# A hybrid decoder step: two small fp32 products written as three products of high and low parts

## The chip, the cores and the metric

The kernel runs on one core of a Trainium2 chip. The metric is the device time of one execution in microseconds (us), the median of the runs of a kernel. Engines are named as the profile names them: PE (TensorE, matmuls), PEld (its weight loads), DVE (VectorE), ACT (ScalarE), POOL (GpSimd), SP (SyncE); ACTq and SPq are the DMA issues of an engine.

## What is computed

One inference step of a decoder with two layers, for 256 tokens of a prompt and 8 single-token requests together: T = 264 columns. The even layer has attention and a short convolution, the odd one gated linear attention and pooling; a SwiGLU block follows each. The change touches two places of the odd layer:

```python
def mixer_odd(h, gla_s0, pool_prev, pool_prev_valid, w_in, w_out, w_alpha_up, b_alpha, gla_gain, w_pool, pool_scale, is_prompt):
    z = h @ w_in
    ...
    zq, zk, zv, zg, zr, zp = jnp.split(z, [o1, o2, o3, o4, o5], axis=-1)
    oc, new_s = gla_mixer(zq, zk, zv, zg, zr, gla_s0, w_alpha_up, b_alpha, gla_gain, is_prompt)
    od, new_pool = pool_mix(zp, pool_prev, pool_prev_valid, w_pool, pool_scale)
    y = jnp.concatenate([oc, od], axis=-1) @ w_out
...
def gla_mixer(zq, zk, zv, zg, zr, s0, w_alpha_up, b_alpha, out_gain, chunked):
    ...
    gk = jax.nn.log_sigmoid((zr @ w_alpha_up + b_alpha).astype(jnp.float32)) / GLA_TAU
...
def pool_mix(u, prev, n_prev, w_pool, scale):
    ...
    for g, w in enumerate(POOL_WINDOWS):
        ...
        outs.append(s / cnt[None, :, None] - ext[:, POOL_BUF:, lo:hi])
    d = jnp.stack(outs, axis=2).astype(u.dtype)
    y = jnp.einsum('btgc,gcd->btgd', d, w_pool).reshape(B, T, POOL_DIM) * scale
```

The gate's up projection is `zr @ w_alpha_up`, 16 to 512. The mix of pooling is the einsum, four groups of 256 to 256.

## The kernel before

**Main products.** All large weights pass in units of two 128-row chunks by 512 columns (`raw`, ring of RING = 4). For each unit ACT copies it to a rounded type (`whi`, fp32r: `split_hi`, L454), DVE subtracts (`wlo` = raw - whi: `split_lo`, L467), and PE does 24 matmuls of 128x128 weights on 264 columns: xh and xl by whi (L583), then xh by wlo (L589). The activations stand as high and low parts too. ACT and DVE split unit n + 3 while PE works on unit n, so they are ahead of PE by AHEAD = 3 units. SP loads unit n when the low part of unit n - 4 is done.

**The odd layer's input projection** is written out by hand as steps s = 0 to 65, each one unit of PE; side work hangs on fixed steps in each engine's own program. Each engine executes its program in order, and semaphores tie them. On PE a step is the unit and then, at some steps: `gate_rank` (s = 10), `dec_outer(s - 40)` (L901, the outer product of a request's key and value, two matmuls), `dec_out` (L911, every second step from s = 42), `pool_mix(c)` (L921, s = 44 to 47 and 52 to 55). On DVE a step is `split_lo`, then `dec_state(s - 40)` (L1720, the state `sgl` of two heads of a request), then the low part of a mix's output (`hl`, L1860) and, at s = 42, 45, 50 and 53, `window_means(g)` (L1735 to L1740), which writes `dmix`. On POOL `window_sums(g)` (L1939) adds the trees of a group's windows: one, two, three and four adds. On ACT a step is `split_hi`, then copies, DMA issues and the high part of a mix's output (`hh`, L1321).

**The two products** are fp32. `gate_rank` multiplies `wup` by `zr` (L813), four matmuls; both have 32 rows, since the 16 columns of the rank stand twice in the weights of steps 8 and 9, as high and low part (is_rank: L449, L464, L957), and `wup` holds the 16 rows twice. `pool_mix` does two matmuls of 128 rows into bank 4, for each of 8 outputs:

```python
                for k in range(2):
                    mm = pe.matmul(ps[:, 4, 0:T], wpool[:, 2 * g + k, m * P:(m + 1) * P], dmix[:, k, :],
                                   start=k == 0, stop=k == 1)
```

The next mix waits for DVE to have taken the last one (pml), and `window_means` of a new group for the mix that reads the old `dmix` (pm_ps).

Of the kernel before, what the change touches and what calls it, by code (L numbers as in the profile page):

```python
# [34 lines left out]
P = 128  # L35
# [99 lines left out]
SGL = 6  # L135


def decoder_step(nc, a, o):
# [6 lines left out]
    with ctx:  # L145
# [92 lines left out]
        zr = put("zr", [32, T], after("attS"))  # L238
        qz = put("qz", [P, GH, NB * NB], after("zr"))
        pst = put("pst", [P, 8, P], after("qz"))  # L240
        assert after("pst") <= end_a, (after("pst"), end_a)
# [19 lines left out]
        wup = put("wup", [32, 512], after("dmix"))  # L261
        sqj = put("sqj", [P, GDV], after("wup"))
        assert after("sqj") <= end_b, (after("sqj"), end_b)
# [73 lines left out]
        gk_ps = sem("gk_ps")  # L337
        zb_ok = sem("zb_ok")
# [91 lines left out]

        def beyond(n, i, step):

            return n + (i * step if isinstance(i, int) else 0) >= U_END

        def split_hi(act, n, i=None, step=0, up=None):
# [12 lines left out]
            if is_rank(n):  # L448
                act.activation(by_rank(whi, n)[:, :, 0:16], by_rank(raw, n)[:, :, 0:16], ACT.Copy).then_inc(hi_done, 1)  # L449
                return  # L450
# [6 lines left out]
        def split_lo(dve, n, i=None, step=0):  # L457
# [4 lines left out]
            if is_rank(n):  # L462
                w = by_rank(whi, n)
                dve.tensor_tensor(w[:, :, 16:32], by_rank(raw, n)[:, :, 0:16], w[:, :, 0:16].bitcast(F32), ALU.subtract).then_inc(lo_done, 1)  # L464
                return
# [101 lines left out]
        def _(pe):  # L567
# [241 lines left out]
            def gate_rank():  # L809
                pe.wait_ge(evac_g, G_ODD + 2)  # L810
                pe.wait_ge(d_odd, 32)
                for h in range(GH):
                    mm = pe.matmul(ps[:, 4 + h, 0:T], wup[:, h * P:(h + 1) * P], zr[:, :], start=True, stop=True)  # L813
# [101 lines left out]
            def pool_mix(c):  # L915
                g, m = divmod(c, 2)
                pe.wait_ge(dmix_ok, g + 1)
                pe.wait_ge(d_wp, 16)
                pe.wait_ge(pml, c) if c else pe.wait_ge(go_ok, 4)
                for k in range(2):  # L920
                    mm = pe.matmul(ps[:, 4, 0:T], wpool[:, 2 * g + k, m * P:(m + 1) * P], dmix[:, k, :],  # L921
                                   start=k == 0, stop=k == 1)
# [22 lines left out]
            for q, (col, s0) in enumerate(zip(ODD_COLS, ODD_FIRST)):  # L945
                G = G_ODD + q
                units = IN_UNITS if col is not None else 2
                for j in range(units):
                    s = s0 + j
                    n = U_ODD + s  # L950
                    if col is None:

                        pe.wait_ge(lo_done, n + 1)
                        for k in range(0, 8, 2):
                            for m, r in enumerate((xh, xl)):
                                for kk in (k, k + 1):
                                    mm = pe.matmul(ps[0:32, 7, 0:T], by_rank(whi, n)[:, kk, 0:32], r[8 * j + kk],  # L957
# [28 lines left out]
                    if 0 <= s - 40 < 16:  # L986
                        dec_outer(s - 40)
                    if s >= 42 and s % 2 == 0 and (s - 42) // 2 < NB:
# [3 lines left out]
                    for half in range(2):  # L992
                        if 44 + 8 * half <= s < 48 + 8 * half:
                            pool_mix(4 * half + s - 44 - 8 * half)
# [8 lines left out]
        def _(act):  # L1003
# [218 lines left out]
            for k in (0, 16):  # L1222
# [32 lines left out]
            for s in range(U_OUT_O - U_ODD):  # L1255
                split_hi(act, U_ODD + s + AHEAD)
                if s == 5:
                    root(2)
                if s == 11:
# [743 lines left out]
```

## Time and profile before

| | us |
|---|---|
| median of 3 runs | 2188.09 (2187.59 to 2188.22) |
| the profiled execution | 2186.03 |
| its span | 2183.9 |
| PE busy in it | 2175.9, 18168 instructions |
| DVE busy | 1211.3 |
| ACT busy | 944.0 |
| POOL busy | 24.3 |

The granted clock of PE is in the top tenth in every slice of the page. A fp32 matmul shows as two PE instructions. The starts of successive matmuls are what counts for PE's time, since the durations of neighbours overlap: matmuls of the main product start 0.12 us apart though one is listed with 0.28 us. The timeline merges alike instructions, and a row's first number is its start.

### The profile page before, as it was taken

What the parts mean: (1) busy time and instruction counts of PE and PEld (TensorE: products, weight loads), DVE (VectorE), ACT (ScalarE), POOL (GpSimd) and SP (SyncE); (2) the same over time, 40 slices, a digit from 0 to 9 for tenths busy, and PEclk for the clock granted to TensorE, in tenths of its full rate; (3) what the DMA queues carried; (4) which work ended last, traced back from release to release, by engine and by line L of the source; (5) the groups of instructions that cost most, each with busy time, mean ns of one, the idle gap of its engine ahead of it and who ended that gap; (6) DMA issues with size and microseconds to landing.
All of it is one profiled execution on the core that took longest, in us unless ns stands there. A gap on an engine that the chain in (4) does not pass through costs nothing.

```text
span 2183.9 us, 43520 instructions
## 1 busy us (share of the span) xinstructions
PE 2175.9 (100%) x18168; PEld 2153.8 (99%) x18168; DVE 1211.3 (55%) x1296; ACT 944.0 (43%) x1055; POOL 24.3 (1%) x35
## 2 busy tenths in 40 slices
PE   9999999999999999999999999999999999999999
PEld 9999999999999999999999899999999999999999
DVE  7777665555555555444465566565555555544443
ACT  7545345443433433443454444454343343433332
POOL 0001000000000000000000020000000000000000
PEclk9999999999999999999999999999999999999999
DMA  7764566566566565556565675556656656566563
GB/s 254 245 171 144 166 184 183 173 193 183 179 185 182 180 185 183 184 176 191 184 204 158 199 234 187 182 171 194 182 180 184 182 180 185 174 192 193 193 191 129
DMA packets 218203, 405.16 MB, mean 186 GB/s; under 512 B 15536, under 2 KB 29616, under 8 KB 217936
## 3 DMA queue, kind: packets, MB, share of 16 engines
q1 hardware_dynamic: 201952, 385.22, 57.5%
q10 hardware_dynamic: 16144, 18.38, 2.5%
q8 instruction: 83, 1.36, 0.2%
q14 instruction: 24, 0.20, 0.0%
HBM read 395.70 MB, written 9.93 MB: 186 GB/s over the span
## 4 chain that ended last, share of the span: by engine, by line
PE 98%; DVE 1%; ACT 1%; DMA 0%; issue 0%; ACTq 0%; DVEq 0%
PE ps L583 63%; PE ps L589 31%; DMA raw<-in_w_in_even 0%; PE ps L921 0%; PE ps L656 0%; PE ps L677 0%; PE ps L666 0%; ACT whi L454 0%; DVE wlo L467 0%; PE ps L874 0%; PE ps L911 0%; PE ps L857 0%; PE ps L878 0%; PE ps L957 0%; PE ps L901 0%
## 5 line engine op out<-in xcount | busy, mean ns | idle before, releaser
L467 DVE TENSOR_TENSOR wlo<-raw,whi 128x1024 fp32r<-128x1024 f32 (+1 forms) x729 | 882.4, 1224 | 788.5 <-ACT whi L454 787.4
L454 ACT ACTIVATE whi<-raw 128x1024 fp32r<-128x1024 f32 (+1 forms) x729 | 761.2, 1055 | 889.2 <-PE ps L589 865.1
L583 PE MATMUL ps<-xh,whi 128*128 128x264 f32 x3904 | 793.6, 284 | 1.0 <-ACT whi L454 1.0
L583 PE MATMUL ps<-xl,whi 128*128 128x264 f32 x3904 | 787.0, 283 | 0.0
L583 PEld LDWEIGHTS ps<-xh,whi 128*128 128x128 f32 x3904 | 599.7, 188 | 9.8 <-issue 6.9
L583 PEld LDWEIGHTS ps<-xl,whi 128*128 128x128 f32 x3904 | 598.9, 188 | 0.0
L589 PE MATMUL ps<-xh,wlo 128*128 128x264 f32 x3904 | 556.5, 283 | 0.0
L589 PEld LDWEIGHTS ps<-xh,wlo 128*128 128x128 f32 x3904 | 504.4, 188 | 0.0
L583 PE MATMUL ps<-hh,whi 128*128 128x264 f32 x1920 | 387.0, 283 | 0.0
L583 PE MATMUL ps<-hl,whi 128*128 128x264 f32 x1920 | 387.0, 283 | 0.0
L583 PEld LDWEIGHTS ps<-hh,whi 128*128 128x128 f32 x1920 | 294.4, 188 | 0.1
L583 PEld LDWEIGHTS ps<-hl,whi 128*128 128x128 f32 x1920 | 294.4, 188 | 0.0
L589 PE MATMUL ps<-hh,wlo 128*128 128x264 f32 x1920 | 270.0, 283 | 0.0
L589 PEld LDWEIGHTS ps<-hh,wlo 128*128 128x128 f32 x1920 | 246.6, 188 | 0.0
L1192 ACT ACTIVATE hh<-ubuf 128x1056 f32 (+1 forms) x22 | 23.9, 1087 | 100.5 <-DVE ubuf L1661 100.5
L1189 ACT ACTIVATE gbuf<-gbuf 128x1056 f32<-128x1056 f32 x22 | 23.9, 1087 | 65.9 <-DVE gbuf L1654 65.9
L1664 DVE TENSOR_TENSOR hl<-ubuf,hh 128x1056 f32 (+1 forms) x22 | 27.7, 1259 | 31.0 <-ACT hh L1192 31.0
L1034 ACT ACTIVATE xh<-x,vec 128x264 fp32r<-128x264 f32 x48 | 20.8, 505 | 36.7 <-DVE x L1624 36.7
L1656 DVE TENSOR_TENSOR ubuf<-ps,rstd 128x1056 f32<-128x1056 f32 x22 | 27.7, 1258 | 12.3 <-PE ps L589 12.3
L1654 DVE TENSOR_TENSOR gbuf<-ps,rstd 128x1056 f32<-128x1056 f32 x22 | 27.7, 1257 | 11.3 <-PE ps L589 11.3
L1380 DVE SCALAR_TENSOR_TENSOR xl<-x,vec,xh 128x264 fp32r<-128x264 f32 x48 | 20.5, 488 | 21.7 <-ACT xh L1034 21.7
L1661 DVE TENSOR_TENSOR ubuf<-ubuf,gbuf 128x1056 f32<-128x1056 f32 x22 | 27.7, 1259 | 2.5
(236 smaller groups left out, 516.2 us busy)
## 6 DMA issues: line engine op xcount, KB each, us to landing
raw<-in_w_gate SPq DMA_DIRECT2D x176, 512.0 KB, 4.0
raw<-in_w_up SPq DMA_DIRECT2D x176, 512.0 KB, 4.3
raw<-in_w_down SPq DMA_DIRECT2D x176, 512.0 KB, 3.9
raw<-in_w_in_even SPq DMA_DIRECT2D x71, 512.0 KB, 4.3
raw<-in_w_in_odd SPq DMA_DIRECT2D x66, 512.0 KB, 3.8
raw<-in_w_out_odd SPq DMA_DIRECT2D x32, 512.0 KB, 4.2
raw<-in_w_out_even SPq DMA_DIRECT2D x16, 512.0 KB, 4.8
raw<-in_w_out_even SPq DMA_DIRECT2D x32, 256.0 KB, 4.2
```

The source lines that it names most:

```text
L454: ins = act.activation(dst, src, ACT.Copy)
L467: ins = dve.tensor_tensor(dst, src, hi.bitcast(F32), ALU.subtract)
L583: pe.matmul(ps[:, bank + t, 0:T], whi[:, s, c:c + P], r[k0 + kk], start=first and kk == 0 and m == 0, stop=False)
L589: mm = pe.matmul(ps[:, bank + t, 0:T], wlo[:, s, c:c + P], yhi[k0 + kk], start=False, stop=last and kk == 1)
L1034: ins = act.activation(xh[c0 + t], x[:, c0 + t, :], ACT.Copy, scale=vec[:, base + c0 + t:base + c0 + t + 1])
L1189: act.activation(gbuf[:, :, :], gbuf[:, :, :], ACT.Silu).then_inc(silu_done, 1)
L1192: act.activation(dst, by_two(ubuf[:, :, :]), ACT.Copy).then_inc(hh_done, 1)
L1380: ins = dve.scalar_tensor_tensor(xl[c], x[:, c, :], vec[:, base + c:base + c + 1], xh[c].bitcast(F32), ALU.mult, ALU.subtract)
L1654: dve.tensor_tensor(gbuf[:, :, :], ps[:, 0:4, 0:T], scale, ALU.mult).then_inc(evac_g, 1)
L1656: dve.tensor_tensor(ubuf[:, :, :], ps[:, 4:8, 0:T], scale, ALU.mult).then_inc(evac_g, 1)
L1661: dve.tensor_tensor(ubuf[:, :, :], ubuf[:, :, :], gbuf[:, :, :], ALU.mult).then_inc(h_ready, 1)
L1664: dve.tensor_tensor(hl[:, at, :, :], by_two(ubuf[:, :, :]), hh[:, at, :, :].bitcast(F32), ALU.subtract).then_inc(hid_done, 1)
```

## The change

- The rank's 16 columns stand three times in steps 8 and 9, each time as high and low part: 96 columns of `whi` instead of 32. `zr` and `wup` have 96 rows (six DMAs of 16 rows instead of two).
- New tiles: `wup3` and `z3` (96 rows, fp32r). ACT copies `wup` and `zr` to them at s = 5 and s = 10 (wu_hi, z_hi), DVE overwrites one third of the rows of each with the low part at s = 6 and s = 10. The gate's four matmuls read these, in fp32r, 96 rows: high by high, low by high and high by low in one product.
- New tiles `wp_hi`, `wp_lo` (the weights of the mix) and `dm_hi`, `dm_lo` (the means). One group of the weights is split at each of s = 43, 44, 48, 49 (POOL_AT and WP_AT); the means at s = 44, 46, 52, 54. Each split is a copy on ACT and a subtraction on DVE, on DVE ahead of `dec_state` of that step.
- A mix is six fp32r matmuls instead of two fp32 ones.
- On PE `pool_mix` stands ahead of `dec_out` of its step, not behind it.

On PE:

```diff
             def gate_rank():
                 pe.wait_ge(evac_g, G_ODD + 2)
-                pe.wait_ge(d_odd, 32)
+                pe.wait_ge(wu_ok, 1)
+                pe.wait_ge(z_ok, 1)
                 for h in range(GH):
-                    mm = pe.matmul(ps[:, 4 + h, 0:T], wup[:, h * P:(h + 1) * P], zr[:, :], start=True, stop=True)
+                    mm = pe.matmul(ps[:, 4 + h, 0:T], wup3[:, h * P:(h + 1) * P], z3[:, :], start=True, stop=True)
...
             def pool_mix(c):
                 g, m = divmod(c, 2)
-                pe.wait_ge(dmix_ok, g + 1)
-                pe.wait_ge(d_wp, 16)
+                pe.wait_ge(dm_ok, g + 1)
+                pe.wait_ge(wp_ok, g + 1)
                 pe.wait_ge(pml, c) if c else pe.wait_ge(go_ok, 4)
-                for k in range(2):
-                    mm = pe.matmul(ps[:, 4, 0:T], wpool[:, 2 * g + k, m * P:(m + 1) * P], dmix[:, k, :],
-                                   start=k == 0, stop=k == 1)
+                for w, d in ((wp_hi, dm_hi), (wp_hi, dm_lo), (wp_lo, dm_hi)):
+                    for k in range(2):
+                        mm = pe.matmul(ps[:, 4, 0:T], w[:, 2 * g + k, m * P:(m + 1) * P], d[:, k, :],
+                                       start=w is wp_hi and d is dm_hi and k == 0, stop=w is wp_lo and k == 1)
```

On ACT:

```diff
-            for k in (0, 16):
+            for k in range(0, 96, 16):
                 act.dma_start(wup[k:k + 16, :], a["w_alpha_up"][0]).then_inc(d_odd, 16)
...
+                if s == 5:
+                    act.wait_ge(d_odd, 16 * 6)
+                    act.activation(wup3[:, :], wup[:, :], ACT.Copy).then_inc(wu_hi, 1)
+                if s == 10:
+                    act.wait_ge(evac_g, G_ODD + 2)
+                    act.activation(z3[:, :], zr[:, :], ACT.Copy).then_inc(z_hi, 1)
...
+                if s in WP_AT:
...
+                    act.wait_ge(d_wp, 16)
+                    act.activation(wp_hi[:, gs, :], wpool[:, gs, :], ACT.Copy).then_inc(wp_h, 1)
+                if s in POOL_AT[::2]:
...
+                    act.wait_ge(dmix_ok, g + 1)
+                    act.activation(dm_hi[:, :, :], dmix[:, :, :], ACT.Copy).then_inc(dm_h, 1)
```

On DVE:

```diff
                 if s == 10:
+                    dve.wait_ge(z_hi, 1)
+                    dve.tensor_tensor(z3[64:96, :], zr[64:96, :], z3[64:96, :].bitcast(F32), ALU.subtract).then_inc(z_ok, 1)
...
+                if s in WP_AT:
...
+                    dve.wait_ge(wp_h, g + 1)
+                    dve.tensor_tensor(wp_lo[:, gs, :], wpool[:, gs, :], wp_hi[:, gs, :].bitcast(F32), ALU.subtract).then_inc(wp_ok, 1)
+                if s in POOL_AT[::2]:
...
+                    dve.wait_ge(dm_h, g + 1)
+                    dve.tensor_tensor(dm_lo[:, :, :], dmix[:, :, :], dm_hi[:, :, :].bitcast(F32), ALU.subtract).then_inc(dm_ok, 1)
                 if 0 <= s - 40 < 16:
                     dec_state(s - 40)
```

DVE at the end of s = 42 to s = 44, of before: the last of the window means (L1740), then for s = 43 and s = 44 a unit's low part (`wlo`) and a state step (`sgl`), then the output of the first mix.

```order
L1740 SCALAR_TENSOR_TENSOR dmix<-small,pst 128x2x8
L467 TENSOR_TENSOR wlo<-raw,whi 128x1024
L1720 SCALAR_TENSOR_TENSOR sgl<-sgl,sqs,ps 128x256 x2
L467 TENSOR_TENSOR wlo<-raw,whi 128x1024
L1720 SCALAR_TENSOR_TENSOR sgl_b<-sgl_b,sqs,ps 128x256 x2
L1860 SCALAR_TENSOR_TENSOR hl<-ps,vec,hh 128x264
```

The same place after the change (L493 is `wlo`, L1763 the state step, L1904 and L1908 the new low parts).

```order
L1783 SCALAR_TENSOR_TENSOR dmix<-small,pst 128x2x8
L493 TENSOR_TENSOR wlo<-raw,whi 128x1024
L1904 TENSOR_TENSOR wp_lo<-wpool,wp_hi 128x512
L1763 SCALAR_TENSOR_TENSOR sgl<-sgl,sqs,ps 128x256 x2
L493 TENSOR_TENSOR wlo<-raw,whi 128x1024
L1904 TENSOR_TENSOR wp_lo<-wpool,wp_hi 128x512
L1908 TENSOR_TENSOR dm_lo<-dmix,dm_hi 128x528
L1763 SCALAR_TENSOR_TENSOR sgl_b<-sgl_b,sqs,ps 128x256 x2
```

Three subtractions stand between the means of group 0 and the point at which PE may read `dm_lo`, and two unit low parts with a state step between them.

DVE at s = 6 to s = 10, of before: the second rank unit's low part, the query's four tiles, low parts, the rank to `zr`, two low parts, and the gate's result.

```order
L464 TENSOR_TENSOR whi<-raw,whi 128x8x16
L1425 TENSOR_TENSOR qg<-ps,rstd 128x264 x4
L467 TENSOR_TENSOR wlo<-raw,whi 128x1024 x2
L1756 TENSOR_TENSOR zr<-ps,rstd 32x264
L467 TENSOR_TENSOR wlo<-raw,whi 128x1024 x2
L1786 TENSOR_SCALAR sqs<-ps,vec 128x264 x4
```

The same place after the change, with the low parts of `wup3` (printed as wup_119) and `z3` (z_103).


```order
L490 TENSOR_TENSOR whi<-raw,whi 128x8x3x16
L1828 TENSOR_TENSOR wup_119<-wup,wup_119 32x512
L1468 TENSOR_TENSOR qg<-ps,rstd 128x264 x4
L493 TENSOR_TENSOR wlo<-raw,whi 128x1024 x2
L1799 TENSOR_TENSOR zr<-ps,rstd 96x264
L493 TENSOR_TENSOR wlo<-raw,whi 128x1024 x2
L1831 TENSOR_TENSOR z_103<-zr,z_103 32x264
L1834 TENSOR_SCALAR sqs<-ps,vec 128x264 x4
```

The new subtraction stands behind the two `wlo`, ahead of the four additions that take the gate's result (L1786, now L1834).

## Rows read from the trace of the kernel before

**Rows 1.** The page, part 1: each engine's busy time, share, instructions.
```profile
PE 2175.9 (100%) x18168; PEld 2153.8 (99%) x18168; DVE 1211.3 (55%) x1296; ACT 944.0 (43%) x1055; POOL 24.3 (1%) x35
```
**Rows 2.** Timeline, PE, s = 10 and the gate: start, duration, engine, line, idle before.
```profile
1125.19 0.41 PE L583 MATMUL ps<-xh,whi 128*128 128x264 f32 x2
...
1128.18 2.04 PE L813 MATMUL ps<-zr,wup 32*128 32x264 f32 x8
...
1133.15 0.40 PE L583 MATMUL ps<-xh,whi 128*128 128x264 f32 x2
```
**Rows 3.** Timeline, ACT and DVE, while PE does s = 10.
```profile
1125.46 1.06 ACT L454 ACTIVATE whi<-raw 128x1024 fp32r<-128x1024 f32 x1 [0.89 <-PE ps L957]
...
1125.75 2.34 DVE L467 TENSOR_TENSOR wlo<-raw,whi 128x1024 fp32r<-128x1024 f32 x2
```
**Rows 4.** Timeline, PE, s = 44 to s = 54: starts of steps, dec_outer, dec_out and mixes.
```profile
1246.93 0.41 PE L583 MATMUL ps<-xh,whi 128*128 128x264 f32 x2
...
1249.82 0.40 PE L901 MATMUL ps<-v,kdiag 72*128 72x256 f32 x2
...
1254.83 1.06 PE L921 MATMUL ps<-dmix,wpool 128*128 128x264 f32 x4
...
1271.53 0.41 PE L583 MATMUL ps<-xh,whi 128*128 128x264 f32 x2
...
1274.75 0.62 PE L911 MATMUL ps<-sgl,qz 128*8 128x256 f32 x8
...
1278.54 0.41 PE L583 MATMUL ps<-xh,whi 128*128 128x264 f32 x2
...
1286.44 1.06 PE L921 MATMUL ps<-dmix,wpool 128*128 128x264 f32 x4
```
**Rows 5.** Timeline, DVE, s = 43 and s = 44.
```profile
1245.78 1.97 DVE L467 TENSOR_TENSOR wlo<-raw,whi 128x1024 fp32r<-128x1024 f32 x1 [0.37 <-ACT whi L454]
1247.67 0.86 DVE L1720 SCALAR_TENSOR_TENSOR sgl<-sgl,sqs,ps 128x256 f32<-128x256 f32 x2
1248.45 1.32 DVE L467 TENSOR_TENSOR wlo<-raw,whi 128x1024 fp32r<-128x1024 f32 x1
```
**Rows 6.** Timeline, POOL, beside Rows 5: the two adds of group 1.
```profile
1245.58 1.09 POOL L1939 TENSOR_TENSOR tree<-ext 128x540 f32<-128x540 f32 x1 [3.12 <-DVE dmix L1740]
1246.74 1.94 POOL L1939 TENSOR_TENSOR tree<-tree 128x536 f32<-128x536 f32 x1
```
**Rows 7.** Groups by form, DVE, 1100 to 1320 us: the subtraction's nearest size.
```profile
L1387 DVE TENSOR_TENSOR sqs<-sqs 128x528 f32<-128x528 f32 x1 | 0.7, 708 | 0.0
```
**Rows 8.** Timeline, DVE, s = 46 and s = 54, the unit's low part.
```profile
1257.96 1.22 DVE L467 TENSOR_TENSOR wlo<-raw,whi 128x1024 fp32r<-128x1024 f32 x1
...
1289.78 1.22 DVE L467 TENSOR_TENSOR wlo<-raw,whi 128x1024 fp32r<-128x1024 f32 x1
```
**Rows 9.** Timeline, DVE, s = 49: low part and state step.
```profile
1271.90 1.22 DVE L467 TENSOR_TENSOR wlo<-raw,whi 128x1024 fp32r<-128x1024 f32 x1
1273.04 0.87 DVE L1720 SCALAR_TENSOR_TENSOR sgl<-sgl,sqs,ps 128x256 f32<-128x256 f32 x2
```
**Rows 10.** Timeline, POOL, s = 49 and s = 52: adds of groups 2 and 3.
```profile
1272.07 1.99 POOL L1939 TENSOR_TENSOR tree<-ext 128x540 f32<-128x540 f32 x1 [23.39 <-DVE pst L1774]
...
1280.71 4.46 POOL L1939 TENSOR_TENSOR tree<-tree 128x536 f32<-128x536 f32 x3
```
**Rows 11.** Timeline, DVE, s = 52: the unit's low part.
```profile
1280.39 1.32 DVE L467 TENSOR_TENSOR wlo<-raw,whi 128x1024 fp32r<-128x1024 f32 x1
```
**Rows 12.** Timeline, the odd layer's start: ACT's DMA issues and first splits.
```profile
1101.21 1.53 ACTq L1235 DMA_DIRECT2D sgl<-in_state_gla  x3
1102.84 2.96 ACT L454 ACTIVATE whi<-raw 128x1024 fp32r<-128x1024 f32 x3 [0.81 <-issue]
```
**Rows 13.** Timeline, PE, start of s = 3 of the odd layer.
```profile
1106.45 0.40 PE L583 MATMUL ps<-xh,whi 128*128 128x264 f32 x2
```
**Rows 14.** Timeline, ACT's DMA issue of a state at s = 44.
```profile
1249.03 1.20 ACTq L1235 DMA_DIRECT2D sgl<-in_state_gla  x1
```

## What the change should do to the time, worked out before it ran

> **What bounds the kernel now.** I read the page's busy times first. PE is busy for 2175.9 of 2183.9 us, in 18168 instructions [rows 1]; that is 0.120 us from one matmul to the next. So PE is the bound everywhere, and what counts of any edit is how long it keeps PE at work or at a wait. I then read the timeline of PE at the two places touched, and beside it DVE, ACT and POOL, since the new products wait for a chain of splits on those. ACT and DVE have spare time on average, but a mean doesn't say whether the split of a value made a moment before is ready when PE arrives; only the order in their queues does.
>
> **The gate, what PE saves.** From the start of unit s = 10 to the start of the unit after s = 11 are 1133.15 - 1125.19 = 7.96 us [rows 2]. Two units of 24 matmuls at 0.12 are 5.76, so the four fp32 matmuls cost 2.20. The four new ones have the form of the main product but for 96 rows; the nearest row with fewer rows, a key-value product of 72 rows, is listed with the same 0.40 for two [rows 4]. I take 0.12 each: 0.48.
>
> **The gate, its new wait.** The unit s = 10 is issued by 1125.19 + 2.88 = 1128.07. DVE's two low parts run to 1125.75 + 2.34 = 1128.09 [rows 3], and the new subtraction on 264 columns stands behind them. Its price: 528 columns take 0.71 [rows 7] and 1024 take 1.22 [rows 8], so about 1.03 ns a column and 0.44 for 264. Successors begin some 0.08 before the listed end of the one ahead (1245.78 + 1.97 against 1247.67 in [rows 5]), so it runs from 1128.01 to 1128.45. ACT's copy to `z3` begins behind its unit at 1126.5 [rows 3] and takes about half of that unit's 1.06, so it is done by 1127.1 and not the last. With 0.1 for the signal and an unhidden weight load (my choice; bounds 0 and 0.3) PE waits 0.5. The gate comes to 1.0 instead of 2.2: **-1.2**.
>
> **The mix, what PE saves.** Steps 44 to 49 take 1271.53 - 1246.93 = 24.60 with four mixes and three dec_out; steps 50 and 51 take 7.01 with one dec_out and no mix [rows 4]. Three times 7.01 is 21.03, so a mix costs 3.57 / 4 = 0.89. Six matmuls at 0.12 are 0.72. Eight mixes save 8 x 0.165: **-1.3**. Moving `pool_mix` ahead of dec_out costs nothing by itself, but the 0.6 of dec_out no longer stands between the unit and the mix, and would have covered as much of each wait below.
>
> **The mix, what it waits for.** The odd mixes of a pair find both operands ready. The first one of each group waits for `dm_lo`. Times are those of the trace of before; a shift of PE moves both sides.
>
> *Group 0, s = 44.* DVE's low part at 1245.78 took 1.97 where the same instruction takes 1.22 elsewhere [rows 5, 8]. POOL's add had started at 1245.58 and ended at 1246.67, and POOL's second add shows 1.94 from 1246.74 but ends 0.93 after DVE's low part, at 1248.68 [rows 6]. So a subtraction and an add that both read SBUF twice exclude each other, and the later one waits: 0.75 here. The Trainium skill says so too (SBUF — State Buffer, Who interferes with whom): a DVE instruction with two SBUF inputs contends with a GpSimd one that reads SBUF, the one issued second blocks until the first is done, and this speaks against new subtractions beside the trees. Now `wp_lo` of group 0 comes at 1247.67, right behind that low part, with POOL's second add already waiting. I take it that POOL goes first. Then `wp_lo` runs effectively from 1248.55, 0.69 long (512 columns), to 1249.24; the state step 0.86 to 1250.02; the low part 1.22 to 1251.17; the second `wp_lo` to 1251.77; `dm_lo` (0.71) to 1252.40, each begun 0.08 early. PE is through its unit and dec_outer at 1249.82 + 0.24 = 1250.06 [rows 4]. Wait 2.34, with 0.15 for signal and load **2.5**.
>
> *Group 1, s = 46.* The chain starts at the mix of s = 45, M = 1254.83 [rows 4], whose end is awaited by ACT and DVE and by the means of group 1. The unit's low part follows at 1257.96 = M + 3.13 [rows 8]. The new mix ends at 0.88 (five starts of 0.12 and 0.28) instead of 1.06, so 0.18 earlier: M + 2.95 to M + 4.17. `dm_lo` ends at M + 4.80. PE is there at M + 0.72 + 2.88 + 0.24 = M + 3.84. Wait 0.96 + 0.15 = **1.1**.
>
> *Group 2, first s = 50.* The fourth `wp_lo` at s = 49 comes at 1273.04, while POOL's first add has been waiting since 1272.07 for the low part of 1271.90 [rows 9, 10]. POOL goes first and is done at 1272.07 + 1.99 = 1274.06; `wp_lo` runs from about 1273.95 to 1274.64, and the state step behind it ends at 1275.42 where it ended at 1273.91. dec_out at 1274.75 needs it [rows 4]: wait **0.75**, on a wait that had 0.8 to spare.
>
> *Group 2, then s = 52.* Now the means are 0.75 ahead of PE, so the low part of the unit isn't held by them but by ACT's own, and I put its end at 1281.2 (at most 1280.39 + 1.32 = 1281.71, as before [rows 11]). POOL's second add for group 3 waits at that moment (before it began at 1280.71 [rows 10]), takes its 0.93, and `dm_lo` runs from 1282.05 to 1282.75. PE is there at 1278.54 + 2.88 + 0.24 = 1281.66 [rows 4]. Wait 1.1 + 0.15 = **1.3**.
>
> *Group 3, s = 54.* As group 1 with M = 1286.44, but the low part stands at 1289.78 = M + 3.34 [rows 4, 8]: wait 1.17 + 0.15 = **1.3**. POOL is done by then.
>
> Sum of the waits: 2.5 + 1.1 + 0.75 + 1.3 + 1.3 = 6.95.
>
> **What is covered.** The four more DMA issues of `wup` stand ahead of ACT's first split of the odd layer. Three issues take 1.53 [rows 12], so four take 2.0 at that pitch, and the split of unit 3 begins at 1104.9 instead of 1102.84 and ends at 1105.9; PE wants it at 1106.45 [rows 13]. It fits, with 0.6 to spare. The wider rank split and the splits of `wup3` lie on engines that are several us ahead of PE there, and `wp_lo` of s = 48 fits into DVE's gap ahead of the state step. I put all of them at nothing; if the cover of the DMA issues fails, it costs what the rival below says. The wider `zr` and the wider rank weights (96 columns where 128 have the same pitch) are nothing either.
>
> **The sum.** -1.2 - 1.3 + 6.95 = +4.4 against the profiled execution's 2186.03: 2190.5. The median of the runs lies 2.1 above that execution, so I forecast 2188.09 + 4.4 = **2192.5**.
>
> **Rivals.**
> *DVE keeps its turn.* If a subtraction that follows another at once goes ahead of POOL's waiting add, `wp_lo` at 1247.67 isn't held. It ends at 1248.36, the state step at 1249.14, the low part (1.32, held a little by the add) at 1250.38, the second `wp_lo` at 1250.99, `dm_lo` at 1251.62: s = 44 waits 1.7. dec_out at s = 50 waits for nothing, and s = 52 for about 1.2 (POOL's adds are later there instead). Waits 1.7 + 1.1 + 1.2 + 1.3 = 5.3, total 5.3 - 2.5 = +2.8: **2190.9**. For it speaks that no row shows two such subtractions in a row with an add waiting, so the order is my inference; against it that in every pair of rows the one that asked first went first.
> *The waits are covered.* If PE finds `dm_lo` ready, only the savings are left, 1.3 + 1.7: **2185.1**. Against it stands that all of DVE's work on the way is listed with its duration; for it only that the chain has many links. It is not a gain that the runs can tell.
> *Slower than this: the DMA issues.* One issue of the same queue took 1.20 [rows 14]. If four 16-row issues took that each, 4.8 in all, the split of unit 3 would end at 1102.84 + 4.8 + 1.06 = 1108.7, 2.2 behind PE's 1106.45: total +6.6, **2194.7**. It decides from 0.64 per issue. Against it: three neighbours took 0.51 each.
>
> **Chances.** The forecast 0.58, DVE keeps its turn 0.22, DMA issues late 0.12, covered 0.04, something else 0.04. About 0.2%, 4.4 us here, is what a measurement can tell from no change, that is 2192.5 at the upper side: the forecast lies on this line, so I give half of its chance to either side. Slower: 0.29 + 0.12 + 0.03 = 0.44. Same: 0.29 + 0.22 + 0.04 = 0.55. Faster by that much has no case, 0.01. The range holds the first two cases with 0.1 to 0.2 of doubt on each of five waits, and most of the third: 2189.9 to 2194.4.
>
> **What would show it.** In the trace after: PE idle ahead of the first mix of s = 44 for 2.3 to 2.6 (1.6 to 1.8 in the rival), of 46, 52 and 54 for 1.0 to 1.4, ahead of one dec_out for 0.7, and ahead of the gate for 0.4 to 0.5, each put down to DVE's `dm_lo`, `sgl` or `z3`; `wp_lo` listed with some 1.6 at s = 43 and s = 49 and 0.7 elsewhere; six mix matmuls 0.12 apart; no idle time at s = 3. Wrong would be a mix without a wait, or a wait on ACT: then my order of links is wrong.

## The result: 8 us slower, more than forecast

| | before, us | after, us |
|---|---|---|
| median of 6 runs | 2187.77 (2187.59 to 2188.22) | 2196.09 (2192.29 to 2198.85) |
| the profiled execution, its span | 2186.03, 2183.9 | 2195.65, 2193.5 |

The ratio is 1.0038, with a 95% interval of 1.0028 to 1.0048. The forecast was 2192.5, in a range of 2189.9 to 2194.4: the sign of the sum was right, its size was not. The changed kernel spreads over 6.6 us, and the six runs of before beside it over 0.6; in the later sessions, with 15 to 27 executions, the kernel before spreads over 3.0 to 3.5 us itself, so at most a spread twice as wide is shown. The changed kernel ran twice more, with 10 and 5 executions; the median of all 21 is 2195.64, 7.8 above the 2187.8 of before.

Parts 1 and 2 of the page after answer to [rows 1]. PE is busy for 3.5 us more and its span is 9.6 longer, so most of the loss is time in which PE stands.

```profile
PE 2179.4 (99%) x18180; PEld 2157.6 (98%) x18180; DVE 1219.9 (56%) x1306; ACT 949.4 (43%) x1065; POOL 25.0 (1%) x35
```

The timeline of PE at the gate and from s = 44 answers to [rows 2, 4] (start, duration, engine, line, names; in brackets the idle time ahead and what ended it; L609 and L615 are the main products, L840 the gate, L928 dec_outer, L938 dec_out, L949 the mix).

```profile
1132.05 0.73 PE L840 MATMUL ps<-z,wup 96*128 96x264 f32 x4 [0.61 <-DVE z L1831]
...
1252.18 0.40 PE L928 MATMUL ps<-v,kdiag 72*128 72x256 f32 x2
1254.79 0.51 PE L949 MATMUL ps<-dm_hi,wp_hi 128*128 128x264 f32 x2 [2.21 <-DVE dm_lo L1908]
1255.14 0.41 PE L949 MATMUL ps<-dm_lo,wp_hi 128*128 128x264 f32 x2
1255.38 0.41 PE L949 MATMUL ps<-dm_hi,wp_lo 128*128 128x264 f32 x2
...
1256.27 0.81 PE L609 MATMUL ps<-xh,whi 128*128 128x264 f32 x2
1256.88 0.64 PE L609 MATMUL ps<-xl,whi 128*128 128x264 f32 x2
1257.32 0.64 PE L609 MATMUL ps<-xh,whi 128*128 128x264 f32 x2
...
1265.94 0.51 PE L949 MATMUL ps<-dm_hi,wp_hi 128*128 128x264 f32 x2 [0.84 <-DVE dm_lo L1908]
...
1282.31 0.62 PE L938 MATMUL ps<-sgl,qz 128*8 128x256 f32 x8 [0.63 <-DVE sgl L1763]
...
1290.46 0.51 PE L949 MATMUL ps<-dm_hi,wp_hi 128*128 128x264 f32 x2 [1.07 <-DVE dm_lo L1908]
...
1300.26 0.51 PE L949 MATMUL ps<-dm_hi,wp_hi 128*128 128x264 f32 x2 [1.05 <-DVE dm_lo L1908]
```

The six waits are where the forecast has them and end by the operations it names. What it doesn't have stands behind the first: successive rows of two matmuls in the next unit start 0.44 us apart (1256.88, 1257.32) instead of 0.24. The windows show it as the granted clock, the column behind POOL's busy time. The first row is of before, the second and third of after:

```profile
1250.00:1300.00 50.00, 50.00 (x402) 44.98 (x402) 34.00 (x67) 18.31 (x25) 11.23 (x7) 1.00 0.86 273
```
```profile
1250.00:1300.00 50.00, 44.47 (x358) 40.71 (x356) 37.98 (x71) 20.18 (x29) 12.94 (x8) 0.97 0.79 254
...
1256.00:1260.00 4.00, 4.00 (x26) 3.73 (x19) 1.72 (x2) 1.26 (x2) 0.00 (x0) 0.57 0.96 329
```

PE stood for 2.2 us, went on at full clock for 1.5, and then had the lower level (granted clock 0.50, that is 1.2 of 2.4 GHz) for the next 3.4.

DVE and POOL answer to [rows 5, 6, 7]: the new low parts, and the two adds of group 1.

```profile
1248.87 1.23 DVE L493 TENSOR_TENSOR wlo<-raw,whi 128x1024 fp32r<-128x1024 f32 x1 [1.10 <-ACT whi L480]
1250.03 1.57 DVE L1904 TENSOR_TENSOR wp_lo<-wpool,wp_hi 128x512 fp32r<-128x512 f32 x1
1251.52 0.86 DVE L1763 SCALAR_TENSOR_TENSOR sgl<-sgl,sqs,ps 128x256 f32<-128x256 f32 x2
1252.30 1.21 DVE L493 TENSOR_TENSOR wlo<-raw,whi 128x1024 fp32r<-128x1024 f32 x1
1253.44 0.68 DVE L1904 TENSOR_TENSOR wp_lo<-wpool,wp_hi 128x512 fp32r<-128x512 f32 x1
1254.04 0.69 DVE L1908 TENSOR_TENSOR dm_lo<-dmix,dm_hi 128x528 fp32r<-128x528 f32 x1
...
1279.89 1.58 DVE L1904 TENSOR_TENSOR wp_lo<-wpool,wp_hi 128x512 fp32r<-128x512 f32 x1
```
```profile
1247.94 1.09 POOL L1996 TENSOR_TENSOR tree<-ext 128x540 f32<-128x540 f32 x1 [3.12 <-DVE dmix L1783]
1249.10 1.94 POOL L1996 TENSOR_TENSOR tree<-tree 128x536 f32<-128x536 f32 x1
```

`wp_lo` takes 1.57 at s = 43 and 1.58 at s = 49, where an add of POOL was waiting ahead of it, and 0.68 at s = 44, where none was. That is the order that the prediction inferred. The place is not the same in every execution, though. In e1, the changed kernel again, ACT's split came later, POOL's second add was already running when the unit's low part came, and the collision fell on that one: 1.86 instead of 1.23, and `wp_lo` behind it was free with 0.68. DVE and POOL there:

```profile
1248.15 1.86 DVE L493 TENSOR_TENSOR wlo<-raw,whi 128x1024 fp32r<-128x1024 f32 x1 [1.64 <-ACT whi L480]
1249.93 0.68 DVE L1904 TENSOR_TENSOR wp_lo<-wpool,wp_hi 128x512 fp32r<-128x512 f32 x1
```
```profile
1247.84 1.08 POOL L1996 TENSOR_TENSOR tree<-tree 128x536 f32<-128x536 f32 x1
```

**Where the time is lost, in numbers.** From the start of dec_outer at s = 44 to that at s = 55 the trace before has 1295.00 - 1249.82 = 45.18 us. The forecast for this stretch, with seven of the eight mixes, is 6.95 - 7 x 0.165 = +5.8. The profiled execution after has +7.39, and the two repeats +10.08 and +10.43. So the executions of one kernel differ here by 3 us, and the experiments ask why.

### The profile page after: what moved, and what is told of

It reads as the page before. It is cut to its first block, busy times and chain, and to the rows that moved or that the text cites. A ratio compares the mean times of both kernels' runs of the same rounds, so it can differ in the third digit from the quotient of the medians.

```text
span 2193.5 us, 43569 instructions
## 1 busy us (share of the span) xinstructions
PE 2179.4 (99%) x18180; PEld 2157.6 (98%) x18180; DVE 1219.9 (56%) x1306; ACT 949.4 (43%) x1065; POOL 25.0 (1%) x35
## 4 chain that ended last, share of the span: by engine, by line
PE 95%; DVE 2%; DMA 1%; ACT 1%; issue 1%; ACTq 0%; POOL 0%; SPq 0%; DVEq 0%; POOLq 0%
PE ps L609 61%; PE ps L615 31%; DMA raw<-in_w_in_even 1%; DVE wlo L493 1%; DMA raw<-in_w_in_odd 1%; ACT whi L480 0%; PE ps L949 0%; PE ps L682 0%; PE ps L703 0%; POOL tree L1996 0%; PE ps L692 0%; PE ps L901 0%; PE ps L884 0%; PE ps L905 0%; DVE dm_lo L1908 0%
## 5 line engine op out<-in xcount | busy, mean ns | idle before, releaser
L493 DVE TENSOR_TENSOR wlo<-raw,whi 128x1024 fp32r<-128x1024 f32 (+1 forms) x729 | 881.7, 1223 | 793.6 <-ACT whi L480 792.4
L609 PE MATMUL ps<-xh,whi 128*128 128x264 f32 x3904 | 796.2, 285 | 0.4 <-ACT whi L480 0.4
L609 PE MATMUL ps<-xl,whi 128*128 128x264 f32 x3904 | 789.8, 283 | 0.0
L609 PEld LDWEIGHTS ps<-xh,whi 128*128 128x128 f32 x3904 | 600.6, 189 | 10.7 <-issue 9.1
L609 PEld LDWEIGHTS ps<-xl,whi 128*128 128x128 f32 x3904 | 600.2, 188 | 0.0
L615 PE MATMUL ps<-xh,wlo 128*128 128x264 f32 x3904 | 556.9, 283 | 0.0
L615 PEld LDWEIGHTS ps<-xh,wlo 128*128 128x128 f32 x3904 | 504.4, 188 | 0.0
L609 PE MATMUL ps<-hh,whi 128*128 128x264 f32 x1920 | 387.5, 283 | 0.0
L609 PE MATMUL ps<-hl,whi 128*128 128x264 f32 x1920 | 387.4, 283 | 0.0
L609 PEld LDWEIGHTS ps<-hh,whi 128*128 128x128 f32 x1920 | 294.2, 188 | 0.1
L609 PEld LDWEIGHTS ps<-hl,whi 128*128 128x128 f32 x1920 | 294.2, 188 | 0.0
L615 PE MATMUL ps<-hh,wlo 128*128 128x264 f32 x1920 | 270.1, 283 | 0.0
L615 PEld LDWEIGHTS ps<-hh,wlo 128*128 128x128 f32 x1920 | 246.5, 188 | 0.0
```

The source lines that it names most:

```text
L493: ins = dve.tensor_tensor(dst, src, hi.bitcast(F32), ALU.subtract)
L609: pe.matmul(ps[:, bank + t, 0:T], whi[:, s, c:c + P], r[k0 + kk], start=first and kk == 0 and m == 0, stop=False)
L615: mm = pe.matmul(ps[:, bank + t, 0:T], wlo[:, s, c:c + P], yhi[k0 + kk], start=False, stop=last and kk == 1)
```

## The experiments

All times are medians of 5 to 11 executions beside the kernel before, whose median was 2187.75 to 2187.91 in the four sessions (e1 to e4; e5 to e7; e8 to e11; e12 and e13). The changed kernel itself had 2193.54 in one session and 2196.91 in another, so differences of less than about 3 us between medians of different sessions say little. "Stretch" is the difference to before from s = 44 to s = 55, as above.

| run | median, us | ratio, 95% | stretch | idle ahead of the mix of s = 44, s = 52 |
|---|---|---|---|---|
| e1 changed kernel again | 2193.54 | 1.0018 to 1.0037 | +10.08 | 2.48, 2.23 |
| e2 gate alone | 2187.11 | 0.9986 to 1.0004 | 0.00 | none |
| e3 pooling alone | 2196.57 | 1.0024 to 1.0048 | +11.69 | 2.48, 3.59 |
| e4 mix behind dec_out | 2191.10 | 1.0009 to 1.0027 | +4.34 | 1.73, 1.69 |
| e5 POOL's adds later | 2191.96 | 1.0010 to 1.0028 | +6.57 | 1.88, 1.35 |
| e6 both DMA pairs later | 2191.22 | 1.0005 to 1.0023 | +4.73 | 1.11, 1.07 |
| e7 gate and mixes later | 2186.69 | 0.9986 to 1.0004 | | none |
| e8 mixes later | 2185.44 | 0.9977 to 0.9995 | | none |
| e9 and z3 first | 2184.67 | 0.9975 to 0.9993 | | none |
| e10 first wait filled | 2196.49 | 1.0023 to 1.0050 | +10.10 | 0.58, 3.62 |
| e11 changed kernel again | 2196.91 | 1.0029 to 1.0056 | +10.43 | 2.48, 2.49 |
| e12 second DMA pair later | 2194.05 | 1.0020 to 1.0041 | +7.60 | 2.48, 1.05 |
| e13 same, wait filled | 2192.91 | 1.0014 to 1.0035 | +6.11 | 0.58, 1.13 |

### The change in its two halves

e1 is the changed kernel unaltered.

> The changed kernel itself, a second time. Waits theory: 2195 to 2196, PE idle about 2.2 us ahead of the first mix of s = 44, 0.8, 1.1 and 1.0 ahead of those of s = 46, 52, 54, 0.6 ahead of the gate and of one dec_out, at the same places again; what lies ahead of the odd layer (3.2 us more than before in the first trace, in code that the change doesn't touch) is chance and should be gone or of another size. Rival, the program as a whole: the 3.2 us ahead of the odd layer are there again.

Its median, 2193.54, is below the 2195 to 2196 expected. It spread from 2192.5 to 2197.9, and its trace has the slow stretch behind s = 44 for longer.

e2 keeps the gate's half only; `pool_mix` is as before and behind dec_out.

```diff
-POOL_AT = (44, 45, 46, 47, 52, 53, 54, 55)
-WP_AT = (43, 44, 48, 49)
+POOL_AT = ()
+WP_AT = ()
```

> The gate's part alone (rank thrice, wup3, z3); pooling's mix is fp32 and behind dec_out, as before. Waits theory: the gate saves 0.9 (four matmuls of 0.12 and a wait of 0.6 in place of 2.2), so 0.9 below the kernel before, about 2186.9, with a spread as small as that of the kernel before (0.6). Rival, any change of the program unsettles its start: 1 to 3 us above the kernel before, spread of some us.

Its row of the gate (PE's timeline):

```profile
1130.71 0.72 PE L840 MATMUL ps<-z,wup 96*128 96x264 f32 x4 [0.44 <-DVE z L1830]
```

From the first rank unit (s = 8) to dec_outer of s = 44 it needs 127.44 us where before needs 128.52: the gate saves 1.08. The median is 0.6 below before, and the interval includes no change.

e3 keeps pooling's half only; `gate_rank`, `zr`, `wup` and their DMAs are as before.

```diff
-                pe.wait_ge(wu_ok, 1)
-                pe.wait_ge(z_ok, 1)
+                pe.wait_ge(d_odd, 32)
                 for h in range(GH):
-                    mm = pe.matmul(ps[:, 4 + h, 0:T], wup3[:, h * P:(h + 1) * P], z3[:, :], start=True, stop=True)
+                    mm = pe.matmul(ps[:, 4 + h, 0:T], wup[0:32, h * P:(h + 1) * P], zr[0:32, :], start=True, stop=True)
```

> Pooling's part alone (split weights and means, six matmuls a mix, mix ahead of dec_out); the rank stands once and the gate is fp32. Waits theory: the five waits less the savings, 5.7, so 2193.5, and 1.5 more where the clock falls behind the long wait of s = 44: 2195.0. If instead the clock falls come from the gate's wait or the front: 2193.5 with a small spread.

It is as slow as the whole change, so the loss is pooling's. In its trace PE waits 3.59 at s = 52, and the clock is low after both long waits.

### What makes the waits

e4 puts `pool_mix` behind dec_out again, as before.

```diff
                         dec_outer(s - 40)
-                    for half in range(2):
-                        if 44 + 8 * half <= s < 48 + 8 * half:
-                            pool_mix(4 * half + s - 44 - 8 * half)
...
                         out_T((s - 60) // 4)
+                    for half in range(2):
+                        if 44 + 8 * half <= s < 48 + 8 * half:
+                            pool_mix(4 * half + s - 44 - 8 * half)
```

> The changed kernel with pool_mix behind dec_out again, as it stood before. Waits theory: dec_out's 0.6 us of work covers as much of each of four waits, so 2.2 to 2.4 below the changed kernel (about 2193.8); 1.5 more below it if the wait at s = 44, then 1.6 instead of 2.2, no longer brings the clock down (2192.3). Rival, the order is of no account because DVE's chain moves along: within 0.5 of the changed kernel.

PE does dec_out while it would have waited, and s = 44 waits 1.73:

```profile
1252.01 0.52 PE L949 MATMUL ps<-dm_hi,wp_hi 128*128 128x264 f32 x2 [1.73 <-DVE dm_lo L1908]
```

No matmul behind it is slow: from the mix's start to the next dec_outer are 1255.74 - 1252.01 = 3.73, the mix and a unit at 0.12 each (3.6) and the step's own 0.1. The order that the prediction put at "costs nothing by itself" is worth 2.4 us beside e1 (2193.5, same session) and 4.5 beside the changed kernel's median over all 21 executions. The cover of 0.6 on each of four waits would be 2.4 already; that the clock stays up is seen in the one trace and is not separable in the medians.

e5 lets POOL's adds wait until the low part beside them is done, so the two never meet.

```diff
                     pool.wait_ge(dmix_ok, g)
+                if g in (1, 3):
+                    pool.wait_ge(dm_ok, g)
+                if g == 2:
+                    pool.wait_ge(wp_ok, 4)
```

> The changed kernel, but POOL's trees of groups 1 and 3 wait until the means of the group before are split (dm_ok), and those of group 2 until all weights are split (wp_ok 4). So no add stands beside the new subtractions. Theory of the shared reads: wp_lo shows 0.7 at s = 43 and s = 49 instead of 1.6, dm_lo 0.7 at s = 52; the waits fall from 2.2 to about 1.0 (s = 44), from 0.6 to 0 (dec_out at s = 50), and about 1 at s = 52; 3 us less in all than the changed kernel, and the clock stays up behind s = 44, 1.5 less again: 2189.5 to 2191. Rival, DVE's queue alone makes the waits: within 1 us of the changed kernel (2193.5 to 2196).

DVE's rows of s = 43 (timeline): neither subtraction is held. The unit's low part starts behind ACT's split after an idle time of 1.68, as in e1 (1.64), and takes 1.23 where e1 has 1.86; `wp_lo` takes 0.69 as there.

```profile
1248.06 1.23 DVE L493 TENSOR_TENSOR wlo<-raw,whi 128x1024 fp32r<-128x1024 f32 x1 [1.68 <-ACT whi L480]
1249.20 0.69 DVE L1904 TENSOR_TENSOR wp_lo<-wpool,wp_hi 128x512 fp32r<-128x512 f32 x1
```

The wait for `sgl` ahead of dec_out at s = 50 (0.63) is gone, and s = 44 is 0.6 shorter than in e1 (1.88, 2.48), the 0.63 that the low part is shorter. This confirms the exclusion as a cause of these waits. The expectation was missed: 2191.96 is above 2189.5 to 2191, and the clock still fell at s = 44. The effect on the median is between 1.6 us (beside e1) and 3.7 (beside all 21 executions), both from other sessions, so its size is open.

e6 moves the two pairs of DMA issues in `pool_rows` (the outputs of pooling's state, `ext` and `pst`) from s = 42 and s = 50 of ACT's program to s = 47 and s = 60.

```diff
-                    if s == 42 + 8 * half:
+                    if s == (47, 60)[half]:
                         pool_rows(half)
```

> The changed kernel, but ACT issues the two pairs of DMAs of pool_rows at s = 47 and s = 60 instead of s = 42 and s = 50. Theory of the uncovered issues (they took 1.0 to 2.7 us a pair from trace to trace, and stand ahead of the splits that the first mixes wait for): the units' low parts at s = 43 and s = 51 start as soon as PE has freed the slot, the wait at s = 52 is 1.1 each time instead of 1.1 to 3.6, median 1 to 1.5 below the changed kernel, and a narrower spread. Rival, the spread is the clock's alone: median and spread as the changed kernel's.

The wait at s = 44 fell to 1.11 from between 2.2 and 2.5, though `wp_lo` took 1.58, and the runs lie closer together (2189.45 to 2192.18). So about half of the longest wait was ACT's: it issues the two DMAs ahead of the split of a unit, the unit's low part on DVE waits for that split, and all new low parts stand behind it. How long an issue takes differs from one execution to the next. First ACT's timeline after, ahead of s = 44 and ahead of s = 52 (L1280 and L1281 are the pair), then the first of the pair ahead of s = 52 in e11 and in e10 (there L1284):

```profile
1245.63 0.58 ACTq L1280 DMA_DIRECT2D out<-ext  x1
1246.24 1.44 ACTq L1281 DMA_DIRECT2D out<-pst  x1
1247.78 1.06 ACT L480 ACTIVATE whi<-raw 128x1024 fp32r<-128x1024 f32 x1 [3.52 <-issue]
...
1283.22 0.52 ACTq L1280 DMA_DIRECT2D out<-ext  x1
1283.78 0.62 ACTq L1281 DMA_DIRECT2D out<-pst  x1
```
```profile
1282.05 2.00 ACTq L1280 DMA_DIRECT2D out<-ext  x1
```
```profile
1280.46 2.40 ACTq L1284 DMA_DIRECT2D out<-ext  x1
```

At s = 52 the pair took 0.52 + 0.62 = 1.14 after (idle 1.07), 0.53 + 1.35 in e1 (idle 2.23), 2.00 + 0.53 in e11 (2.49), 2.40 + 0.53 in e10 (3.62).

### What the clock costs

In e10 PE does 16 more matmuls ahead of the first mix, on 256 columns each, whose result is overwritten; the mix can't start earlier by that.

```diff
+                pe.wait_ge(pml, c) if c else pe.wait_ge(go_ok, 4)
+                if c == 0:
+                    pe.wait_ge(wp_h, 1)
+                    for k in range(16):
+                        pe.matmul(ps[:, 4, 0:256], wp_hi[:, k % 2, 0:P], wp_hi[:, 0, 0:256], start=True, stop=True)
                 pe.wait_ge(dm_ok, g + 1)
                 pe.wait_ge(wp_ok, g + 1)
-                pe.wait_ge(pml, c) if c else pe.wait_ge(go_ok, 4)
```

> The changed kernel, and ahead of the first mix, while PE would wait for the low part of the means, 16 matmuls (128x128 on 256 columns, their result overwritten) of 0.12 us each, 1.9 us in all. Nothing is taken off the path: dm_lo comes when it comes. Theory (the clock falls because PE stood still): the wait of 2.2 to 2.5 becomes 0.3 to 0.6 behind the filling, the granted clock stays at full level and the eight slow pairs behind the mix are gone: 1.5 below the changed kernel run beside it, about 2193. Rival (the clock falls for another reason, as what ACT, DVE and POOL do at that place, or would have risen anyway): slow pairs behind the mix as before and no difference, or slower by what the filling overshoots, 0 to 0.3.

> The changed kernel itself once more, beside the one with the filled wait: 2193.5 to 2196 by its earlier runs. Both theories: waits of 2.2 to 2.5 at s = 44, with a clock fall behind it of about 1.5, and of 1.0 to 3.6 at s = 52, as ACT's DMA issues fall.

In the traces the theory holds: in both the mix starts 2.88 us after dec_outer, and from there to the next dec_outer are 4.46 in e10 and 5.91 in e11. The medians, 2196.49 and 2196.91 with five executions each, don't show 1.5. The wait at s = 52 of e10's profiled execution was 1.1 longer than e11's, and it had the low clock behind it in both. So e10 alone settles nothing about the median, and the swing of s = 52 had to be taken out: e12 moves only the second pair of issues (s = 50 to s = 60), e13 does that and fills the first wait as e10 does.

```diff
-                    if s == 42 + 8 * half:
+                    if s == (42, 60)[half]:
                         pool_rows(half)
```

> The changed kernel with only the second pair of pool_rows' DMA issues moved, from s = 50 to s = 60 on ACT; the first pair stays at s = 42. Theory (an issue of 0.5 to 2.2 us ahead of ACT's split makes the wait of s = 52 swing between 1.1 and 3.6; the wait of 2.2 to 2.5 at s = 44 and the clock behind it come from the first pair): wait at s = 52 steady at 1.1 with no clock fall, wait at s = 44 of 2.2 to 2.5 with eight slow pairs: 2193.5 to 2194.5, between the changed kernel (2195.6 over 21 runs) and the one with both pairs later (2191.2). Rival (the second pair doesn't matter): 2195.6.

> The same with the 16 matmuls that fill the wait of s = 44. Everything that swings is out of it, so the median must show the clock's price alone. Theory (the clock falls because PE stands still there): no slow pairs behind the first mix, 1.5 below the kernel beside it, or more where that one's clock stays low longer. Rival (the clock's fall at s = 44 costs nothing that counts in the median, because it happens in few executions, or the time comes back later): the same median within 0.3.

PE in e12, then in e13, from the first mix on:

```profile
1250.53 0.40 PE L928 MATMUL ps<-v,kdiag 72*128 72x256 f32 x2
1253.41 0.51 PE L949 MATMUL ps<-dm_hi,wp_hi 128*128 128x264 f32 x2 [2.48 <-DVE dm_lo L1908]
...
1255.57 0.64 PE L609 MATMUL ps<-xl,whi 128*128 128x264 f32 x2
1256.01 0.64 PE L609 MATMUL ps<-xh,whi 128*128 128x264 f32 x2
...
1259.42 0.41 PE L928 MATMUL ps<-v,kdiag 72*128 72x256 f32 x2
```
```profile
1250.52 0.40 PE L928 MATMUL ps<-v,kdiag 72*128 72x256 f32 x2
1250.76 2.06 PE L948 MATMUL ps<-wp_hi 128*128 128x256 f32 x16
1253.40 0.51 PE L953 MATMUL ps<-dm_hi,wp_hi 128*128 128x264 f32 x2 [0.58 <-DVE dm_lo L1912]
...
1255.22 0.41 PE L609 MATMUL ps<-xl,whi 128*128 128x264 f32 x2
1255.46 0.41 PE L609 MATMUL ps<-xh,whi 128*128 128x264 f32 x2
...
1257.86 0.41 PE L928 MATMUL ps<-v,kdiag 72*128 72x256 f32 x2
```

The mix starts at the same time, and the next dec_outer is 1.56 later where PE had stood still. The spans differ by 1.5 (2192.1, 2190.6), the medians by 1.14 (2194.05, 2192.91; 8 runs each, which overlap). That PE's standing still is the cause is shown by the rows: the clock fell there in all five traces with a wait of 2.2 to 2.5 at s = 44 and in neither of the two with the wait filled. In the median the sign is as expected, but with runs that overlap the size is not shown: 1.1 is the best guess, and 1.5 is not excluded.

With the second pair of issues moved, e12's trace has 1.05 at s = 52 and e13's 1.13. e12's median is 1.6 below the changed kernel's 2195.64 and 0.5 above that of e1, so no gain is shown in the median.

### Work that needn't be waited for

In e7 the mixes and their splits are taken apart by a step or more, and the gate goes from s = 10 to s = 11.

```diff
-POOL_AT = (44, 45, 46, 47, 52, 53, 54, 55)
-WP_AT = (43, 44, 48, 49)
+MIX_AT = (45, 46, 48, 49, 53, 54, 56, 57)
+DM_AT = (44, 47, 52, 55)
+WP_AT = (43, 45, 46, 48)
...
-                    if s == 10:
+                    if s == 11:
                         pe.wait_ge(std_done, 3)
```

> All of the change, with a step of room for each chain: the gate at s = 11 instead of 10, the mixes at s = 45, 46, 48, 49, 53, 54, 56, 57, the means' splits at 44, 47, 52, 55, the weights' at 43, 45, 46, 48. Waits theory: no wait is left, so the savings alone, 1.7 for the gate and 1.3 for the mixes: 2184.8, 3.0 below the kernel before, with its spread. Rival, the fp32r forms themselves or the moved work cost something that I have not seen: 2187 or more.

The median, 2186.69, is above the 2184.8 expected. No mix waits, and the clock stays up in the odd layer. But a new wait appears some 19 us behind the gate:

```profile
1151.11 0.48 PE L610 MATMUL ps<-xh,whi 128*128 128x264 f32 x2 [1.80 <-DVE kg L1470]
```

The gate a step later makes all that follows from it on ACT and DVE later, up to the scaled key (`kg`). e8 leaves the gate at s = 10. e9 also lets ACT copy `zr` ahead of its unit's split, and DVE subtract ahead of the unit's low part:

```diff
+                if s == 10:
+                    act.wait_ge(evac_g, G_ODD + 2)
+                    act.activation(z3[:, :], zr[:, :], ACT.Copy).then_inc(z_hi, 1)
                 split_hi(act, U_ODD + s + AHEAD)
...
+                if s == 10:
+                    dve.wait_ge(z_hi, 1)
+                    dve.tensor_tensor(z3[64:96, :], zr[64:96, :], z3[64:96, :].bitcast(F32), ALU.subtract).then_inc(z_ok, 1)
                 if q is None:
                     split_lo(dve, U_ODD + s + AHEAD)
```

> The mixes stand at s = 45, 46, 48, 49, 53, 54, 56, 57 and their splits are moved with them, the gate stands where it does in the changed kernel. Theory (what costs is the waits for the low parts and the clock that falls after the longest of them): no wait ahead of any mix, the 1.8 us wait for kg at s = 17 that the later gate had made is gone, the gate's own wait of 0.44 is back; so 1.3 below the run with gate and mixes late (2186.7): about 2185.4, 2.4 below before, with no clock fall in the odd layer. Rival (the time is lost in the input of the layer or by the fp32r products themselves): 2186.7 or more, as the run before it, with the same rows at the mixes.

> As the kernel with late mixes, and at s = 10 ACT copies the rank to its high part ahead of its unit's split, and DVE subtracts ahead of the unit's low part. Theory: the 0.44 ahead of the gate is gone and nothing else is late, since both engines are a unit or more ahead: 0.4 below the kernel with late mixes, about 2185.0. Rival: the unit's splits, now 0.4 later on each engine, come late for PE at s = 11 to 13 or for the gate's exp chain; then a wait appears there and the time is that of the kernel with late mixes or more.

Both came out near what was expected, 2185.44 and 2184.67. PE's gate in e9 has no wait, and a mix of the late ones is a row without brackets right behind dec_outer:

```profile
1129.74 0.65 PE L841 MATMUL ps<-z,wup 96*128 96x264 f32 x4
...
1253.79 0.41 PE L929 MATMUL ps<-v,kdiag 72*128 72x256 f32 x2
1254.03 0.41 PE L950 MATMUL ps<-dm_hi,wp_hi 128*128 128x264 f32 x2
```

From the rank to dec_outer of s = 44 are 1249.80 - 1123.00 = 126.80, 1.72 less than before: to the hundredth the 2.20 - 0.48 that the prediction had for the gate without its wait. e9 is 3.2 us below before (ratio 0.9984, 0.9975 to 0.9993), the best of all kernels here. The prediction's rival "the waits are covered" has 3.0 of saving; e9 is that case. It differs from e8 by 0.8 with runs that overlap, so that step of it is shown in the trace and not in the median.

## Why the prediction was wrong

**Right: what the new products cost PE.** Mix matmuls start 0.12 apart; the gate, free of its wait, saved 1.72 as worked out.

**Right: the waits and who ends them.** Counted as in the prediction, from 0.24 after dec_outer's start, the execution after has 2.37 at s = 44 (forecast 2.5), 1.00 at s = 46 (1.1), 0.79 at dec_out (0.75), 1.23 at s = 52 (1.3) and 1.21 at s = 54 (1.3). The sum is 6.60, forecast 6.95. Nothing waits at s = 3, so the issues of `wup` are covered; that rival is out. "DVE keeps its turn" is out by `wp_lo`'s 1.57: POOL's add was there at 1249.10, `wp_lo` came at 1250.03 and waited. Here this trace agrees with the Trainium skill (SBUF — State Buffer, Who interferes with whom), by which the one issued second blocks.

**Right by luck: the size at s = 44.** The forecast had the unit's low part of s = 43 begin 4.04 ahead of dec_outer, as before, and held by POOL to 1.97. In the trace after ACT's two issues let it begin 0.73 later (1248.87, 3.31 ahead of 1252.18), and it then took 1.23, 0.74 less. So `wp_lo` came when the forecast said, 2.15 ahead of dec_outer, for another reason. In e1, e11 and e12 the issues were longer still, `wp_lo` took 0.68, and the low part ahead of it was the one held (1.75 to 2.00); the wait was 2.48. That ACT has a part in this wait is not in the prediction.

**Slightly off: the gate.** It saved 0.87 in the first trace and 1.08 in e1, e2 and e11, where 1.2 was forecast. The listed wait is 0.44 to 0.61, but beside e9, which has none, e2 loses 0.64 where 0.44 is listed and 0.5 was forecast.

**The step that failed first: no term for the clock.** The prediction priced a wait by its length and held all matmuls behind it at 0.12. Its own page before showed PE at full clock in every slice, and in that trace PE had one long wait, in the even layer, behind which the clock stayed up, so nothing there priced a fall. That row, of before:

```profile
63.53 1.16 PE L630 MATMUL ps<-sqs,cst 128*128 128x264 f32 x4 [3.13 <-DVE sqs L1553]
```

Behind the wait at s = 44 the clock cost 1.57 in the trace after, 2.86 in e1, 1.45 in e11 and 1.55 in e3, each as the time from the mix's start to the next dec_outer less the 4.46 of e13. For the profiled execution the sum gave 2190.5, and 2195.65 were measured: of the 5.1 between them 1.6 is this, 0.3 is the gate, and 3.2 lie ahead of the changed code (the last point below). Of the 3.4 by which the median over all executions exceeds the forecast rise (7.8 against 4.4), the three traces of the changed kernel would give it 2.5 in the mean, both waits counted; the one pair of medians that isolates the first wait, e12 and e13, differs by 1.1.

**The step that failed second: one trace's issues taken for all.** For s = 52 the prediction put the end of the unit's low part at "ACT's own" pace, 1281.2, and had only the issue durations of one execution. In the first trace after they happened to be as short and the wait came out as forecast, 1.23. In e1 it was 2.39 and in e11 2.65, the latter with another 1.48 for the clock behind it. Over the three traces of the changed kernel the stretch is +9.3 in the mean where +5.8 was forecast; with the gate's 1.0 that gives +8.1 with the eighth mix, and the medians differ by 7.8. The range left this out although [rows 14] show an issue with 1.20: that row was used for the start of the layer only, where there was cover, and not for s = 42 and s = 50, where there was none.

**The step that hid both: "moving pool_mix ahead of dec_out costs nothing by itself".** It named the 0.6 of cover on each wait and counted it in, but that 0.6 also bears on whether the clock falls behind the longest wait: it is 1.73 in e4, where dec_out covers it and the clock stayed up, and 2.2 to 2.5 without that cover, where it fell.

**Not of the change.** The first rank unit started at 1121.30 in the trace before and at 1124.53 after, 3.2 of the 9.6 us between the spans. It started at 1123.37 in e2 and at 1125.40 in e8, which are no slower than before, so it moves from execution to execution. Nor does the new code on the way cost anything: from the first matmul behind the even layer's wait to the first rank unit the trace before needs 1057.77 us, and e4 and e6, where the clock stayed up too, need 1057.78 and 1057.77. In the trace after, 1.5 of the 3.2 is the clock behind the even layer's wait and the rest lies ahead of that wait. The clock fell there in the profiled executions after, e1 to e3, e5, e8 to e10, e12 and e13, and not in before, e4, e6, e7 and e11. The profiled execution of before was one without the fall, and the forecast's step from it to the median (2.1) takes care of that.

## What to carry over

A wait on the bounding engine had two prices here, its length and what the clock took behind it; when waits near 2 us are forecast, the range must hold the second. A change in order that covers 0.6 us of each of four waits was worth 2.4 us or more. Where a chain of small splits hangs on an engine that also issues DMAs, take the issues' durations from several places, since one took four times as long as another here, and move issues that nobody waits for behind the chain. The finer products paid here only with their operands split a step before use: the same change with the mixes one or two steps later is faster than both kernels.

## What the runs showed of the hardware

The granted clock fell at times from 0.4 us before PE took up work again (e1, at s = 44) to 1.7 us after (e3, at s = 44). It went to 0.50 and stayed there for 3.4 us, and in e1 for 6.8. Two windows of e1 show it lower while PE still stood (PE's busy time, the second number, is 0.00, and the clock, third from the end, 0.73), and at 0.50 when PE went on:

```profile
1253.00:1253.80 0.80, 0.00 (x0) 0.00 (x1) 0.80 (x3) 0.00 (x0) 0.00 (x0) 0.73 0.95 224
1253.80:1254.30 0.50, 0.50 (x2) 0.50 (x3) 0.50 (x2) 0.00 (x0) 0.00 (x0) 0.50 1.10 295
```

In the odd layer it fell with idle times of 1.88 (e5), 2.21 and 2.48 (after, e1, e3, e11, e12), 2.49 (e11, s = 52), 3.59 (e3) and 3.62 (e10). It did not with 1.73 and 1.69 (e4), 1.80 (e7) and 2.23 (e1, s = 52), and with the 3.1 us wait of the even layer it fell in ten of fifteen traces. So length alone doesn't decide, and what else does stays open.

A DVE subtraction that follows directly on another one with which POOL's add had collided let that add go first: `wp_lo` took 1.57 at s = 43 and 1.58 at s = 49 instead of 0.68. The issue of the `ext` output on ACT took 0.50 (e5) to 2.40 us (e10) at s = 42 and s = 50, and held all that stood behind it on that engine.
